# Mixture of experts on one core: the small token set's gate and up product in one group behind the large set's product, instead of one group behind each half

## What is computed

```python
    xe = hf[idx]                                   # per expert: 128 sample rows, 64 prompt rows, of 1024 numbers
    a = jnp.einsum('ecd,edf->ecf', xe, w_gate)     # w_gate, w_up: 16 x 1024 x 512
    u = jnp.einsum('ecd,edf->ecf', xe, w_up)
    ye = jnp.einsum('ecf,efd->ecd', jax.nn.silu(a) * u, w_down)   # w_down: 16 x 512 x 1024
    ye = gates[..., None].astype(ye.dtype) * ye
    out = jnp.zeros_like(hf).at[idx].add(ye)
```

## Time and profile before

| | |
|---|---|
| median of 3 runs | 1623.55 us (1623.14 to 1625.81) |
| the profiled execution | 1623.36 us, span 1621.5 us |
| TensorE busy | 1447.0 us, 89% of the span |
| VectorE busy | 932.7 us |
| ScalarE busy | 721.8 us |
| the stage of the experts | from 946.8 to about 1438 us of the span, 16 passes |

### The profile page before, as it was taken

The page is one execution under the profiler, slowest core; times in us unless marked ns, Lnnn a source line. Parts: engine busy times, 40 slices in busy tenths (PEclk is TensorE's granted clock), DMA queues, the critical chain, the costliest instruction groups (busy, mean ns, idle before and its releaser), DMA issues. The chain is left out here.

```text
span 1621.5 us, 21520 instructions
## 1 busy us (share of the span) xinstructions
PE 1447.0 (89%) x7320; PEld 1016.2 (63%) x7320; DVE 932.7 (58%) x1324; ACT 721.8 (45%) x1157; POOL 182.2 (11%) x255
## 2 busy tenths in 40 slices
PE   5999997599999969869998969999999999948997
PEld 4777775365565535458887746666666666627885
DVE  5444443377677748723347856677676676643553
ACT  4333433376666747722221544444444444423332
POOL 1111111000000000010000111112112121021110
PEclk9999998699999979989998979999999999978999
DMA  8533322713111054064432756878878788753331
GB/s 257 94 111 110 110 97 85 252 64 114 70 63 55 20 190 156 29 208 156 140 123 87 262 169 220 263 252 270 256 261 267 254 262 265 245 164 126 126 135 65
DMA packets 118847, 261.53 MB, mean 161 GB/s; under 512 B 7648, under 2 KB 37472, under 8 KB 115720
## 3 DMA queue, kind: packets, MB, share of 16 engines
q1 hardware_dynamic: 110592, 233.55, 41.2%
q0 software_dynamic: 7168, 25.17, 6.7%
q10 hardware_dynamic: 1032, 2.10, 1.1%
HBM read 194.20 MB, written 66.58 MB: 161 GB/s over the span
## 5 line engine op out<-in xcount | busy, mean ns | idle before, releaser
L1742 DVE TENSOR_TENSOR moe_w_lo<-ring,moe_w_hi 128x2048 fp32r<-128x2048 f32 x96 | 220.3, 2296 | 163.5 <-ACT moe_w_hi L1681 163.4
L1681 ACT ACTIVATE moe_w_hi<-ring 128x2048 fp32r<-128x2048 f32 x96 | 183.7, 1914 | 204.0 <-PE moe_p_g L1864 82.2
L1413 PE MATMUL mix_p_big<-kept_out_w,mix_m_hi 128*128 128x512 f32 x384 | 126.4, 411 | 4.6 <-DVE mix_m_lo L1288 2.4
L510 PE MATMUL proj_p_out<-proj_w_hi,proj_h_hi 128*128 128x512 f32 x264 | 110.8, 420 | 9.5 <-DVE proj_q_hl L408 9.5
L1872 PE MATMUL moe_p_gu<-ring,moe_xT_r 128*64 128x512 f32 x512 | 116.9, 598 | 0.0
L510 PE MATMUL proj_p_out<-proj_w_lo,proj_h_hi 128*128 128x512 f32 x264 | 105.0, 398 | 0.0
L510 PE MATMUL proj_p_out<-proj_w_hi,proj_h_lo 128*128 128x512 f32 x264 | 104.9, 397 | 0.0
L962 DVE TENSOR_REDUCE sample_ntop<-sample_p_s 128x1 f32<-128x1024 f32 x64 | 78.2, 1222 | 37.4 <-PE sample_p_s L784 36.7
L798 PEld LDWEIGHTS sample_p_t<-sample_ident_r,sample_probs_r 128*128 128x128 f32 x688 | 73.1, 142 | 23.2 <-ACT sample_probs L900 6.6
L1413 PEld LDWEIGHTS mix_p_big<-kept_out_w,mix_m_hi 128*128 128x128 f32 x384 | 73.1, 196 | 21.4 <-issue 2.6
L798 PE MATMUL sample_p_t<-sample_ident_r,sample_probs_r 128*128 128x128 f32 x688 | 80.1, 246 | 5.0 <-ACT sample_probs L900 2.5
(11 more groups left out here) (298 smaller groups left out, 3122.4 us busy)
## 6 DMA issues: line engine op xcount, KB each, us to landing
ring<-in_w_gate SPq DMA_DIRECT2D x32, 1024.0 KB, 5.6
ring<-in_w_up SPq DMA_DIRECT2D x32, 1024.0 KB, 7.6
ring<-in_w_down SPq DMA_DIRECT2D x32, 1024.0 KB, 7.2
qT_d<-proj_qT SPq DMA_DIRECT2D x12, 1024.0 KB, 3.9
sample_q<-qT_d SPq DMA_DIRECT2D x8, 1024.0 KB, 5.3
proj_x<-in_x SPq DMA_DIRECT2D x12, 512.0 KB, 4.3
proj_w_raw<-in_w_in SPq DMA_DIRECT2D x8, 768.0 KB, 5.6
kT_d<-proj_kT SPq DMA_DIRECT2D x12, 512.0 KB, 3.6
```

Source lines behind the costliest of these rows:

```text
L510: last = pe.matmul(p_out[:, cols], h[:, s, k, :], w[:, k, cols], start=(k == 0 and n == 0), stop=(k == KC - 1 and n == 2))
L1413: mm = pe.matmul(p_out[:, cols], m[:, s, k, :], ww[:, k, cols], start=(k == 0 and n == 0), stop=(k == KC - 1 and n == 2))
L1681: act.activation(w_hi[:, at % SPLIT], raw[:, at % RAW], ACT.Copy).then_inc(hi_made, 1)
L1742: dve.tensor_tensor(w_lo[:, at % SPLIT], raw[:, at % RAW], w_hi[:, at % SPLIT].bitcast(F32), ALU.subtract).then_inc(lo_made, 1)
```

## The change

Before, the prompt's product of half 0 stands behind the sample's product of half 0, and that of half 1 behind that of half 1. In the changed kernel both prompt products stand behind the sample's product of half 1. The number of instructions, their shapes and sums are the same.

```diff
                     sample((p_g, p_u)[j % 2][:], at, xT_hi, xT_lo, half * FC, half == 0, half == 1)
-                if half == 0 and later(e, 1):
-                    pe.wait_ge(mul_made, e * 2)
-                prompt(p_gu, at - 1, xT_r, half * FC, half == 0, half == 1)
+                if half == 1:
+                    if later(e, 1):
+                        pe.wait_ge(mul_made, e * 2)
+                    prompt(p_gu, at - 3, xT_r, 0, True, False)
+                    prompt(p_gu, at - 1, xT_r, FC, False, True)
```

## The result

| | before | changed |
|---|---|---|
| median of 6 runs | 1626.17 us (1623.14 to 1626.83) | 1664.72 us (1661.95 to 1666.31) |
| ratio | | 1.0241, 95% interval 1.0227 to 1.0254 |
| profiled execution, span | 1621.5 us | 1663.4 us |
| mean granted clock of TensorE | 0.947 | 0.938 |

The changed kernel is 2.4% slower, by some 39 us. That is the forecast direction and inside the range of 1641 to 1668, but 13 us above the predicted 1652. The prediction worked from the profiled execution, so its change is best held against the profiles: 28.5 us were forecast, and the span grew by 41.9.

A forecast was written before the change was run, and what follows sets the result against it. TensorE was taken to set the pace in the experts' stage. Expert 0's 4.4, the passes' 21.0 and expert 15's 1.5 us on 1623.4 gave 1650.3; one clock fall of 1.6 made it 1652, range 1641 to 1668.

The forecast's parts named there:

- The wait: TensorE ahead of turn_x_prompt (L1840) waits 1.7 us for x_low; net + 1.5 us a pass, experts 1 to 14, 21.0 us.
- The forecast itself: Experts' stage: waits of 1.3 to 1.9 us and none to five falls of the clock, 1643 to 1660 us; 74%.
- if the clock is low in many passes: Named sign of being wrong, for TensorE's clock in the experts' passes; the forecast took one fall in all.
- The gain: On TensorE, one prompt group fewer between sample matmuls saves 0.20 us a pass, 3.2 us over 16.
- The clock: TensorE's clock behind the new waits: one fall in all, + 1.6 us, between none and one at each of 14 passes.
- the clock falls at each wait: Rival: TensorE's clock falls in each of 14 passes, 14 x 1.6 us more, 1672.7 us; 9%.
- the second rival: Second in the prediction's list: TensorE's wait and gain cancel within 0.2% (3.2 us), no difference; 3%.
- Expert 0: First pass: turn_x_prompt moves from 971.32 to 975.7, + 4.4 us, idle from 2.48 to about 7, nothing added for the clock.
- Expert 15: Last pass: its down units come later, so TensorE begins at T + 32.0 instead of T + 30.5, + 1.5 us.
- all cover holds: Rival: in the experts' stage the transfer is early enough, only 0.2 us a pass counts, 1620.2 us, faster; 6%.
- The transfers did not bind: Against the rival that transfers bind: gate unit takes 7.5 us instead of 5.5, each pass loses 2.0 more, 1680 us; 8%.
- the first rival: First in the prediction's list, for the experts' stage: all cover holds, 1620.2 us; 6%.

The follow-up runs named there:

- The late release alone: Kernel before with its matmul order, but SyncE issues half 0's gate and up units only after the sample's product of half 1; 1667.64 us, ratio 1.0257.
- the later split: Changed kernel with split 6 on ScalarE and VectorE behind the prompt's silu and multiply and the next sample rows' taking out; 1619.08 us, ratio 0.9956.

## Why the prediction was right, and what was off

- **The wait.** The step "it waits 1.7 us where it did not wait at all" held: issue at T + 15.0, landing 5.5 us later, 14 waits of 1.7 to 2.0 us, and 31.6 us for a pass without a fall, all as worked out. The late release alone and the later split show it as the cause.
- **How it landed in the range.** The forecast itself allowed none to five falls of the clock and spanned 1643 to 1660. The runs had eight falls, and 1664.7 lies above that span. It is inside 1641 to 1668 only through the margin added for milder forms of the rivals. One sign of being wrong that the prediction named, "if the clock is low in many passes", came true.
- **The gain.** The 0.20 us a pass was too small: the group behind both halves saves 0.43 (29.68 against 30.11), the one between them 0.32. I had priced only the changes between kinds of matmul, and these are 0.26 (the sample's two halves take 11.08 us with the later split, 5.68 + 5.66 before); beside it one group of 32 records takes 7.02 us (1188.57 to 1195.59), where two of 16 take 2 x 3.58. As the chain sets the pass, the gain goes into the wait (1.9 for 1.7) and not into the time.
- **The clock.** This is the term that was mis-sized. I took one fall, 1.6 us. There were seven in the passes of experts 2 to 14 and one in that of expert 1 (0.78 from 1005 to 1010 us), and each made a pass 1.7 us longer (33.3 against 31.6): 8 x 1.7 = 13.6 us, 12 more than I took, and nearly all of the 13 us that the prediction was short of. The size of one fall, 1.6, was right; their number was a guess between two rows, and what decides it in a pass isn't shown by any run. The rival "the clock falls at each wait" was half right.

  The loop that the Trainium skill describes (TensorE: Matmul & The Clock Gate, section "HAM oscillation — how this bites in real kernels") is throttled in every pass; here it was so in 8 of 14. That loop waits about 3 to 5 us in each pass, so it says nothing firm of waits of 1.7 to 2.0. The prediction calls the time by that rule that of the second rival; it is the third of its list, 1672.7.
- **Expert 0.** Its pass grew by 4.7 us in the profile (31.5 against 26.8), for 4.4. Behind the longer wait the clock was low for longer too, 0.61 from 980 to 985 us against 0.86 from 975 to 980 before, for which I had added nothing: expert 1's pass has 0.9 us more than its own wait and fall explain, though the two profiles of before differ by 1.5 in the same pass. The part end to end isn't settled beyond 1 to 6 us.
- **Expert 15.** The wait ahead of its down product grew from 1.8 to 2.9 us. In its pass that product began at T + 31.2, against T + 30.5 before: 0.7 us for the 1.5 forecast.
- **The other rivals.** That all cover holds is refuted by the waits. The transfers did not bind: the gate unit landed after 5.5 us, and with the later split a pass took 29.7 us. The words "no wait of TensorE stands in this stage now" under the first rival hold for experts 1 to 14 only: the earlier trace rows have 2.48 us for expert 0 and 1.79 for expert 15.

The changed kernel against the one before, by profile: 4.7 for expert 0, 14 x 1.5 = 21 for the waits, 13.6 for the clock, which is 39.3 of the 41.9 us between the two spans. The rest is the stage's start, 0.6 later, the 0.9 of expert 1's pass, and about 1 at the end.

## What to carry to other kernels

When work is moved behind other work, look at the signals that it raises as well as at its own place: here a product that nobody waited for carried the release of two ring slots, and the transfer behind that release stood at the head of two in-order engines. Measure the slack of each hand-over (2.0 us here) against the delay (5.5 us, of which the quicker landing gave 2.0 back) before counting the gain (0.4 us). The better cure was not to give the signal back early but to take the waiting split out of the way of the work that TensorE needs next: with it the changed kernel is 0.4% faster than the one before, about half of which the kernel before gets from that placing alone.

## What the runs showed of the hardware

- Waits of equal length had different costs: of 1.95 and 1.94 us in one kernel, one was followed by a lower clock and the other not. Of 14 waits of 1.7 to 2.0 us, 8 were; of 14 of 1.0 to 1.4 us at the same place, none; of 14 of 0.9 to 1.3 us between the short transposes (L1855), four. What decides between them isn't shown.
- A full clock was kept by matmuls of no use: 1.9 us of them in each wait made the changed kernel 11 us faster.
- The prompt matmul has 64 columns. In the kernel two alternate between the halves of the output's partitions, and a record costs 0.22 us (16 in 3.58). Three instructions for one half alone took 2.79 us for 6 records, 0.47 each, twice as much. That they run side by side only when they go to different halves fits this. But the three also write the same output and each starts its sum anew, and which of the two costs the time was not tested.
